# Moving the last 320 token columns of 16 merge-gate blocks from the input projection into the attention phase

## The reference

```
z = layer_norm(x) @ w_in + b_in        # queries, keys, values, gates, and 3 * 1024 merge-gate columns
o_nsa = g0*compressed + g1*selected + g2*window   (4 heads of 64)
o_ml  = mLSTM read-out                            (4 heads of 64)
o_fox = softmax(q k + sum of log forget) v        (4 heads of 64)
y = sum over the 3 branches of sigmoid(merge_m) * (o_m @ w_branch_m)
x = LayerNorm(alpha*x + y @ w_out);  x = LayerNorm(alpha*x + top-1 group, top-2 expert MLP(x))
```

## Time and profile before

| | us |
|---|---|
| three runs | 1518.65, 1515.13, 1517.9 |
| median | 1517.9 |
| the profiled execution: its own time | 1516.69 |
| its span, first to last instruction | 1515.1 |
| mean granted TensorE clock in it | 0.953 |

### The profile page before, as it was taken

The page is one execution under the profiler, slowest core; times in us unless marked ns, Lnnn a source line. Parts: engine busy times, 40 slices in busy tenths (PEclk is TensorE's granted clock), DMA queues, the critical chain, the costliest instruction groups (busy, mean ns, idle before and its releaser), DMA issues. The chain is left out here.

```text
span 1515.1 us, 23746 instructions
## 1 busy us (share of the span) xinstructions
PE 1367.6 (90%) x8917; PEld 1185.1 (78%) x8917; DVE 613.6 (41%) x1593; ACT 506.6 (33%) x953; POOL 352.7 (23%) x454
## 2 busy tenths in 40 slices
PE   5999999999999999978889878979985999999945
PEld 3999999999898989956565657968874888888812
DVE  6222212212323224044677547854562333333318
ACT  5422221222122221126555545530012334333233
POOL 5211150020102000003333214621133222323202
PEclk9999999999999999969999989989986999999967
DMA  7244393162625224781004027752126788887755
GB/s 210 69 157 146 124 241 119 58 182 71 183 64 150 73 68 70 189 224 22 1 2 160 19 82 241 259 177 82 51 93 173 246 279 265 286 276 250 263 201 203
DMA packets 188963, 228.31 MB, mean 151 GB/s; under 512 B 47606, under 2 KB 157302, under 8 KB 187486
## 3 DMA queue, kind: packets, MB, share of 16 engines
q1 hardware_dynamic: 176270, 186.25, 40.7%
q0 software_dynamic: 12592, 40.71, 8.6%
HBM read 167.89 MB, written 60.19 MB: 151 GB/s over the span
## 5 line engine op out<-in xcount | busy, mean ns | idle before, releaser
L1255 PE MATMUL psum<-proj_x_hi,proj_w_hi 128*128 128x362 f32 (+1 forms) x1056 | 357.6, 339 | 1.2 <-POOL proj_x_lo L1461 0.8
L1255 PE MATMUL psum<-proj_x_hi,proj_w_lo 128*128 128x362 f32 (+1 forms) x1056 | 347.0, 329 | 0.0
L1255 PE MATMUL psum<-proj_x_lo,proj_w_hi 128*128 128x362 f32 (+1 forms) x1056 | 347.0, 329 | 0.0
L1255 PEld LDWEIGHTS psum<-proj_x_hi,proj_w_hi 128*128 128x128 f32 x1056 | 199.7, 189 | 8.2 <-issue 2.2
L1255 PEld LDWEIGHTS psum<-proj_x_lo,proj_w_hi 128*128 128x128 f32 x1056 | 199.9, 189 | 0.0
L1255 PEld LDWEIGHTS psum<-proj_x_hi,proj_w_lo 128*128 128x128 f32 x1056 | 199.5, 189 | 0.0
L1380 DVE TENSOR_TENSOR proj_w_lo<-proj_w_raw,proj_w_hi 128x1024 fp32r<-128x1024 f32 x44 | 54.0, 1228 | 271.1 <-ACT proj_w_hi L1288 271.0
L1317 ACT ACTIVATE proj_sig<-psum,proj_bias 128x362 f32<-128x362 f32 (+1 forms) x72 | 40.4, 563 | 241.3 <-PE psum L1255 232.2
L2666 PEld LDWEIGHTS psum<-moe_xgt,expert_gate_w 128*128 128x128 f32 x512 | 83.2, 190 | 13.2 <-issue 13.2
L2666 PE MATMUL psum<-moe_xgt,expert_gate_w 128*128 128x192 f32 x512 | 90.1, 329 | 0.7 <-ACT moe_xgt L2710 0.7
L2666 PE MATMUL psum<-moe_xgt,expert_up_w 128*128 128x192 f32 x512 | 88.4, 326 | 0.0
(11 more groups left out here) (473 smaller groups left out, 2386.0 us busy)
## 6 DMA issues: line engine op xcount, KB each, us to landing
proj_w_raw<-in_w_in SPq DMA_DIRECT2D x43, 512.0 KB, 5.2
expert_gate_w<-in_moe_w_gate SPq DMA_DIRECT2D x16, 1024.0 KB, 5.8
expert_up_w<-in_moe_w_up SPq DMA_DIRECT2D x16, 1024.0 KB, 11.1
expert_down_w<-in_moe_w_down SPq DMA_DIRECT2D x16, 1024.0 KB, 8.0
merge_sig<-gate_scratch SPq DMA_DIRECT2D x24, 544.0 KB, 4.1
gate_scratch<-proj_sig SPq DMA_DIRECT2D x48, 181.0 KB, 2.0
final_pair<-expert_rows SPq DMA_DIRECT2D x8, 1024.0 KB, 11.6
feature_scratch<-proj_feat SPq DMA_DIRECT2D x13, 512.0 KB, 3.0
```

The lines of the kernel that those rows point to most:

```text
L1255: mm = nc.tensor.matmul(k.ps[u % RING][:, 0:w], b[wt][:, x % 2, kk, :], b[xx][:, kk, a0:a0 + w], start=(kk == 0 and i == 0), stop=(kk == K ...
```

## The change

Of the last 16 of the 24 merge-gate blocks (`EARLY = 8`) only the first two token chunks are still projected in `project`. The third chunk is projected in `attention`. The chunks are now 384, 384 and 320 columns wide everywhere, the merge included. `project` has 44 * 3 - 16 = 116 units. The third chunk of `x_hi` and `x_lo` lies in tiles of its own (`late`) that live until attention is over.

Attention gets 32 lots, two per block, each of 4 feature tiles times three products: 12 matmuls of 320 columns in PSUM bank 7. They stand at the steps v = -1, 0, 2, 3, 5, 6, ... 45, cut into four parts of three matmuls: behind the first chunk of `scores(v+2)`, behind its last, behind `turn(v)` groups 0 and 1, and behind `values(v-1)`. A lot's weights (256 KB) are loaded again by SP, rounded by ACT (`gate_high`) at the start of the step that follows lot h-2, two steps ahead of its own, and their rest is taken by POOL (`gate_low`) in the same step, ahead of `ratios`. ACT evacuates a block in the step after its second lot (`gate_out`), and SP stores it.

To make room, all values of a unit go to bank 6, `values(u)` waits for `outputs(u-1)` and no longer for `outputs(u-2)`, fox values take the space of the mLSTM's, some tiles share space, the mLSTM's results are stored tile by tile, and the loads of the fox values are issued later, with the other fox loads.

The decode steps are placed in half units: a step is emitted ahead of a unit (on PE in its middle, ahead of feature tile 4) or after it, and each step has a length of 1, 2 or 3 halves. The transposes of the cached pages are mixed with the state steps. They start at unit 66, and "last" stands at half 210, which is ahead of unit 105 of 116.

```diff
-MCH = [(0, 364), (364, 362), (726, 362)]
+MCH = [(0, 384), (384, 384), (768, 320)]
+LATE = 2
+EARLY = 8
+LATE_AT, LATE_W = MCH[LATE]
...
-STEPS = (["turn_cmp0", "turn_cmp1", "sums", "cmp0", "rows", "cmp1", "ends", "cmp2", "bounds", "cmp3"] + ["state0", "state1", "gap0", "state2", "gap1", "state3"]
...
+STEPS = ([("turn_cmp0", 2), ("turn_cmp1", 2), ("sums", 2), ("cmp0", 1), ("rows", 1), ("cmp1", 1), ("ends", 1), ("cmp2", 1), ("bounds", 1), ("cmp3", 2),
+          ("state0", 2), ("state1", 2), ("turn0_0", 2), ("state2", 2), ("turn1_0", 2), ("state3", 2), ("turn2_0", 1), ("turn3_0", 2)]
+         + [(f"{x}_0", n) for x, n in zip(GROUP_STEPS, (2, 1, 2, 1, 1, 2))] + [("ml_s_0", 2), ("ml_t_0", 1), ("ml_v_0", 2), ("ml_s_1", 2), ("ml_t_1", 1), ("ml_v_1", 3), ("out_0", 1)]
+         + [("turn0_1", 1), ("turn1_1", 1), ("turn2_1", 1), ("turn3_1", 2)] + [(f"{x}_1", n) for x, n in zip(GROUP_STEPS, (2, 1, 2, 1, 1, 2))]
+         + [("out_1", 2), ("new_s", 1), ("new_g", 1), ("new_w", 2)] + [(f"up{x}", 2) for x in range(4)] + [("last", 1)])
-SIDE_FROM = 67
+SIDE_FROM = 66
...
-    units = [(0, 0), (1, 0), (0, 1), (1, 1), (0, 2), (1, 2)] + [(x, n) for x in range(2, NB) for n in range(3)]
+    units = [(0, 0), (1, 0), (0, 1), (1, 1), (0, 2), (1, 2)] + [(x, n) for x in range(2, NZ) for n in range(3)] + [(x, n) for x in range(NZ, NB) for n in range(3 if x - NZ < EARLY else LATE)]
...
+    KH = KD // 2
+    NG = 3 * KD - EARLY
+    lot_steps = [v for v in range(-1, 47) if (v + 1) % 3 != 2][0:2 * NG]
+    lot_at = dict(zip(lot_steps, range(2 * NG)))
+    made_at = {-2: [1]} | {lot_steps[h - 2] + 1: [h] for h in range(2, 2 * NG)}
+    out_at = {lot_steps[2 * g + 1] + 1: g for g in range(NG)}
...
+            def gate(v, m0, m1):
+                if v not in lot_at:
+                    return
+                h = lot_at[v]
+                if m0 == 0:
+                    pe.wait_ge(s["g_lo_done"], h + 1)
+                    if h % 2 == 0 and h >= 2:
+                        pe.wait_ge(s["g_evac"], h // 2)
+                for m in range(m0, m1):
...
+                    mm = nc.tensor.matmul(k.ps[7][:, 0:LATE_W], b[wt][:, h % 2, j, :], late[xx][:, kk, :], start=(kk == 0 and i == 0), stop=(kk == KD - 1 and i == 2))
...
                     mm.then_inc(s["scores_mm"], 1)
+                    if c == 0:
+                        gate(u - 2, 0, 3)
...
-                if u >= 2:
-                    pe.wait_ge(s["out_done"], u - 1)
+                if u >= 1:
+                    pe.wait_ge(s["out_done"], u)
...
                 if v + 2 < NU:
                     scores(v + 2)
+                else:
+                    gate(v, 0, 3)
+                gate(v, 3, 6)
                 if 0 <= v < NU:
                     turn(v, range(min(2, ngroups[v])))
+                gate(v, 6, 9)
                 if v >= 1:
                     values(v - 1)
+                gate(v, 9, 12)
...
+            def gate_low(h):
+                pool.wait_ge(s["g_hi_done"], h + 1)
+                nc.gpsimd.tensor_tensor(b["g_lo"][:, h % 2], b["g_raw"][:, h % 2], b["g_hi"][:, h % 2].bitcast(F32), ALU.subtract).then_inc(s["g_lo_done"], 1)
...
+            gate_low(0)
             for v in steps:
+                for h in made_at.get(v, ()):
+                    gate_low(h)
                 if 0 <= v < NU:
                     ratios(v)
...
+            def gate_high(h):
+                act.wait_ge(s[f"g_raw{h % 2}"], 16 * (h // 2 + 1))
+                if h >= 2:
+                    act.wait_ge(s["g_mm"], h - 1)
+                nc.scalar.copy(b["g_hi"][:, h % 2], b["g_raw"][:, h % 2]).then_inc(s["g_hi_done"], 1)
...
+                nc.scalar.activation(b["g_sig"][:, g % 2, :], k.ps[7][:, 0:LATE_W], ACT.Identity, bias=late["bias"][:, EARLY + g:EARLY + g + 1]).then_inc(s["g_evac"], 1)
...
             for v in steps:
+                if v in out_at:
+                    gate_out(out_at[v])
+                for h in made_at.get(v, ()):
+                    gate_high(h)
                 if 0 <= v < NU:
                     copies(v)
...
+                for h in made_at.get(v + 1, ()):
+                    if 2 <= h + 1 < 2 * NG:
+                        sp.wait_ge(s["g_lo_done"], h)
+                        gate_weights(h + 1)
```

207 lines of the change are left out of this document (134 added, 73 removed).

## The result

The changed kernel takes 1547.6 us, the median of 1539.1, 1547.6 and 1556.0 us, against 1518.3 us for the kernel before on the same chip: a ratio of 1.0206, with a 95% interval of 1.0173 to 1.0239. A fourth execution took 4115 us at full granted clock; nothing here explains it, and it is left out of every number. The same kernel measured again, beside other experiments, gave 1553.4 us and 1.0242 (1.0197 to 1.0287). By the mean of the two ratios it is slower by 34 us; the prediction was 1503 us, with 1525 us as the upper end.

The account below looks back on a forecast made before the run. PE was taken to bound projection and attention, with 28 us of room in attention. Terms -57.2 + 57.2 - 19 - 4 + 10 + 0.3, plus 1.7 of small items, gave -14 us: 1503 us, range 1492 to 1513 (1482 to 1525 with rivals).

Parts of the forecast that it names:

- Matmul prices, blocks with three chunks, 16 short blocks: Projection: 175.4 ns for 384 columns, 148.9 for 320; three-chunk blocks unchanged, 16 short blocks save 57.2 us.
- What is late next is a block's weights ... 0 to +2: Projection: 512 KB of weights now needed every 8.4 us instead of every 12, priced at 0 to +2 us.
- Decode steps: Projection: decode steps packed into 50 units instead of 64, priced at 0, with -5 and +8 us as ends.
- The end of the projection: Last decode stores and loads before attention: 10 us of slack stay of 15, priced at 0.
- the rival of the tail: Decode's last stores and loads take over 10 us more, attention starts late: some +8, 1511 us; chance 0.08.
- The loads of lots go over queues that are idle from 704 us on: Attention: lots' weight loads meet idle queues (DMA share 0.00); loads ahead of attention's others cost 0 to +2 us.
- ACT and POOL: Attention: rounding on ACT and subtraction on POOL ahead of the ratio delay PE's transposes, +10 us, ends +2 and +35.
- the rival with 2.63 us: Attention: POOL's subtraction takes 2.63 us, not 1.38, so 30 steps lose a further 1.0 us each; 1534 us, chance 0.10.
- Attention, PE's new work, +57.2 us: Attention: 32 lots of 12 matmuls at 148.9 ns each add 57.2 us to PE.
- Attention, what hides them, -19: Attention: lots fill two thirds of PE's 28.2 us of waits, -19 us, with 10 and 28 as ends.
- Attention, the clock, -4: Attention: fewer PE pauses behind the ramp mean less time at 1.2 GHz, -4 us, ends 0 and -12.
- Single bank and merge: Attention's values waiting for the previous unit's outputs cost +0.3 us; the merge's new chunks 0, ends +2.5 and -4.

Follow-up runs that it names:

- k1: h4 with the eight state stores issued one by one over eight half steps, not in pairs over four; 1501.9 us, 0.9916 of the kernel before.
- f6: Changed kernel with three load/store orders on SP altered: lots 2 and 3 weights earlier, fox loads spread, state stores spread; 1524.4 us, ratio 1.0085.
- f5: The changed kernel measured again with no edit; 1553.4 us, 1.0242 of the kernel before.
- f7: f6 with POOL computing a step's ratio ahead of the lot's subtraction, not behind it; 1510.9 us, 0.9962 of the kernel before.
- g1: f7 with each lot's twelve matmuls at one place behind the scores, not in four parts; 1510.4 us, 0.9968 of the kernel before.
- h4: f7 with each lot in two parts of six matmuls, behind the scores and between transposes and values; 1509.3 us, 0.9941 of the kernel before.
- h1: The kernel before with one edit of the change: values of all units summed in one PSUM bank; 1516.2 us, ratio 0.9991.
- e3: Changed kernel with the decode's four pairs of small state stores issued over four half steps, not in one block; 1542.8 us, ratio 1.0177.
- e1: Changed kernel with the weights of lots 2 and 3 fetched amid attention's first loads, not behind them; 1531.4 us, ratio 1.0095.

## Why the prediction was wrong, step by step

- **Matmul prices, blocks with three chunks, 16 short blocks: right.** 173 and 147 ns. (The sum for the old blocks has 166.5 ns, where the earlier trace rows give 166.3; it changes nothing.) The projection's work fell by 58.6 us, predicted 57.2. In k1, where no load is late, the last product is at 588.9 us, inside the 588 to 592 of the forecast.
- **"What is late next is a block's weights ... 0 to +2": failed.** The weights were late by 5.3 us, in the repeat by 6.2. I compared ACT's and DVE's time for a block with its 8.4 us, but not the time to landing with small stores ahead: SP's rows from 595.72 on stood in the earlier trace rows, with a weight load in the same queue, and in 12 us a block could bear it. The projection's waits grew from 7.9 to 13.2 us, and its clock cost from 1.5 to 6.2, a term that I had left out for this phase. With 1.4 us more work gone than predicted these make the 8.7 us. In k1 the two are 6.6 and 1.5.
- **Decode steps: right**, 0 within what the gaps show (3.0, 1.8 us after; 1.6, 2.3, 2.3 before). **The end of the projection, and the rival of the tail: right and out.** The barrier's gap is 4.45 us against 4.33 in the earlier trace rows; the sign "above 4.3 us" was drawn so tightly that it tells nothing.
- **"The loads of lots go over queues that are idle from 704 us on": the step that failed most.** It looked at one window of the earlier trace rows and left out its neighbours: 652 to 704 us, with a DMA share of 0.67, where lot 2's load had to pass, and 767 to 834 us with 0.26, the fox loads. And it asked whether the queue has bandwidth, not what is issued ahead of the load. SP is in order, so lot 2's load waited behind 8 MB for a place. I had written that the ramp hides a load of 256 KB ahead of the others; the load behind them was not priced at all. Cost: 16.1 + 8.4 us of gaps and the clock behind them, 27 us of attention (f6 against f5).
- **ACT and POOL: the mechanism and the size were right, +10 us.** In f6, without late loads, PE waits 10.8 us for the ratio and f7 takes out 11.3 us of attention. The subtraction took 1.27 us (1.26 to 1.49), predicted 1.38; the rival with 2.63 us is out. What I missed is the coupling: the subtraction that waits for a load keeps the ratio behind it, so the order on POOL and the order on SP multiply. Of my signs of being wrong, "waits of PE for `ratio` of over 20 us" came, with 33.3 us.
- **Attention, PE's new work, +57.2 us: too small.** The work grew by 65.8 us. The intervals of 384 matmuls sum to 73 us, since every part of three pays about 0.1 us at each change of tile shape. Joining parts did not pay, though (g1, h4).
- **Attention, what hides them, -19: 13 to 18 us, and outweighed by the gaps.** The waits of the change are 15.7 us more than before, but without the two gaps (15.8 and 8.1) and the 9.4 us of short waits for the ratio they are 17.6 us less. In f7 they are 13.3 us less.
- **Attention, the clock, -4: the wrong sign.** It cost 1.5 us more than before; the stretch of 626.9 to 647.4 us, which begins in the ramp's gap, is the longest at the lower level. In f7, where that gap is gone, it costs 7.8 us less, and behind the ramp the granted clock is 1.00 against 0.92, 1.00, 0.97 in the earlier trace rows:

```profile
655.00:886.50 231.50, 221.05 (x1882) 164.69 (x1882) 128.88 (x554) 128.26 (x313) 93.11 (x151) 1.00 0.27 74
```

- **"Matmuls take double there": nearly.** 267 against 147 ns for 320 columns, 1.8 times.
- **Single bank and merge: right**, 0 (h1). Behind attention the profiled execution of the change lost 4.7 us more; 4.5 us of that is PE's one long wait for the gather of the experts' inputs, 6.8 us against 2.3. In the other executions it goes from under 0.7 us (f7) to 8.3 (e3), and what sets it is open.

The sum in the profiled execution: predicted 1502.7, measured 1556.0, 53 us apart. 8.7 us are the projection, 4.7 us the stages behind attention, and 38.4 us attention (327.0 against 244.1 + 44.5). Attention's share by the split: 8.6 us more work than predicted, 24.4 us more waits (+15.7 against -19 + 10 + 0.3), and 5.5 us more clock. The side of the result came from the loads and the ratio together: with both mended, by orders that move no work between engines, the same change is faster than the kernel before (f7, k1).

That k1's 1501.9 us lies beside the forecast of 1503 is luck in part. Its attention is 43.6 us longer than before, 44.5 predicted, by 56.7 of work, -8.4 of waits and -4.6 of clock; but its ratio comes first, so the +10 is missing in it, and it hides 8.4 us where the forecast had 19; and its lots have two parts, not four. Two errors of 10 us cancel.

No rival named had this mechanism. The rival that did end on the right side, slower by the ratios, had the right releaser, the wrong price (2.63 us) and not the reason.

## What to carry to other kernels

When a change adds a transfer, find the instruction that issues it and list what the same queue issues in the 20 us ahead, in bytes and in packets; a mean DMA share of a neighbouring window does not show it. Price a pause of PE at more than its length: the clock fell behind it, and e1 gained 20 us from a gap of which 12 went. On an in-order engine, put the operation that somebody waits for ahead of the one that is made in advance, above all when the latter can wait for a load: here two swapped lines were worth 24 of 34 us. A wait names the last link; follow it back until something did real work or was issued late. And where matmuls are cut to price them, look at the granted clock: here up to 40 of 56 us came back as waits and lower clock.

## What the runs showed of the hardware that was not expected

- Between matmuls of different tile shapes (128*128, 64*128, 128*64) PE loses about 0.1 us at each change, between equal shapes nothing: 250 and 240 ns against 147 ns.
- A weight load of 512 KB landed 14.4 us after its issue behind nine small state stores; between 535 and 575 us the quickest took 3.9 us.
- PE's clock and waits explain nearly all that attention's length differs by between executions of the same matmuls: 265.4 to 265.9 us of work in six traces of 298 to 327 us.
- POOL's subtraction of 512 columns, 1.27 us in the median, took 2.23 us in e1 where it ran beside a 1.23 us DVE operation with two inputs from SBUF, and 1.48 to 1.49 us beside a short one of the same kind. That is what the prediction had looked for in the spread of L1461. The two rows of e1:

```profile
615.83 1.23 DVE L1978 TENSOR_TENSOR attn_cmp_s<-attn_cmp_s,attn_cmp_sum 128x1024 f32<-128x1024 f32 x1
615.97 2.23 POOL L2019 TENSOR_TENSOR attn_g_lo<-attn_g_raw,attn_g_hi 128x512 fp32r<-128x512 f32 x1 [9.31 <-ACT attn_g_hi L2131]
```
